# Second feed-forward of a two-block transformer: four pairs of weight chunks in seven products instead of three, their weight sums kept in DRAM

## What is computed

```
def sq_relu_mlp(h, w1, w2):                     # first block
    return jnp.square(jax.nn.relu(h @ w1)) @ w2
...
        merged = jax.nn.sigmoid(ga) * (y_a @ w_up_a[layer]) + jax.nn.sigmoid(gb) * (y_b @ w_up_b[layer])
        x = x + merged @ w_out[layer]
        h = rmsnorm(x, norm_ffn[layer])
        x = x + (jax.nn.silu(h @ w_gate[layer]) * (h @ w_up[layer])) @ w_down[layer]
    return rmsnorm(x, norm_final)
```

## Time and profile before

| | us |
|---|---|
| median of 3 runs | 718.4 (718.36 to 718.87) |
| the profiled execution | 718.42 |
| its span | 716.3 |
| TensorE busy / VectorE / ScalarE / GpSimd | 706.7 / 574.6 / 429.9 / 34.5 |

### The profile page before, as it was taken

How to read it: one execution, slowest core, us unless ns; L and a number is a source line. 1 busy time by engine, 2 the same in 40 slices (tenths; PEclk the granted TensorE clock), 3 DMA queues, 4 the chain that set the end, 5 groups by cost and what they waited for, 6 DMA issues and landing times.

```text
span 716.3 us, 9684 instructions
## 1 busy us (share of the span) xinstructions
PE 706.7 (99%) x3710; PEld 565.7 (79%) x3710; DVE 574.6 (80%) x972; ACT 429.9 (60%) x704; POOL 34.5 (5%) x55
## 2 busy tenths in 40 slices
PE   8999999999999999999999999999999999999996
PEld 4678885578888888888888777777888888888885
DVE  4789999899677868686998799855857789888883
ACT  3477658996745635646545677767447654754652
POOL 1030012001100100000010000000000000000000
PEclk9999999999999999999999999999999999999999
DMA  9996939617778975747538533336463894976901
GB/s 368 414 374 222 389 102 358 230 59 262 272 246 311 337 281 203 258 154 291 164 113 295 209 118 118 118 130 214 128 234 128 315 329 169 332 258 227 354 2 59
DMA packets 72109, 163.76 MB, mean 229 GB/s; under 512 B 4272, under 2 KB 15536, under 8 KB 70528
## 3 DMA queue, kind: packets, MB, share of 16 engines
q1 hardware_dynamic: 68016, 149.47, 58.8%
q0 software_dynamic: 3760, 13.42, 5.2%
q10 hardware_dynamic: 288, 0.27, 0.1%
HBM read 157.90 MB, written 5.24 MB: 228 GB/s over the span
## 4 chain that ended last, share of the span: by engine, by line
PE 95%; issue 1%; DVE 1%; ACT 1%; POOL 0%; POOLq 0%; DVEq 0%
PE bank L570 23%; PE bank L572 23%; PE bank L571 23%; PE bank L915 6%; PE bank L552 5%; PE bank L913 3%; PE bank L589 1%; PE bank L644 1%; PE bank L652 1%; PE bank L647 1%; PE bank L1047 1%; PE bank L1069 1%; PE bank L753 1%; PE bank L629 1%; PE bank L775 1%
## 5 line engine op out<-in xcount | busy, mean ns | idle before, releaser
L1791 DVE TENSOR_TENSOR WL<-W,WH 128x1024 fp32r<-128x1024 f32 (+2 forms) x240 | 270.4, 1172 | 25.6 <-ACT WH L1247 25.2
L1247 ACT ACTIVATE WH<-W 128x1024 fp32r<-128x1024 f32 (+2 forms) x240 | 228.6, 1013 | 63.4 <-DMA W<-in_w_mlp 38.1
L570 PE MATMUL bank<-WH,AHL 128*128 128x512 f32 (+1 forms) x420 | 165.2, 393 | 0.0
L572 PE MATMUL bank<-WH,AHL 128*128 128x512 f32 (+1 forms) x420 | 162.0, 386 | 0.0
L571 PE MATMUL bank<-WL,AHL 128*128 128x512 f32 (+1 forms) x420 | 161.8, 385 | 0.0
L570 PEld LDWEIGHTS bank<-WH,AHL 128*128 128x128 f32 x420 | 78.9, 188 | 18.2 <-issue 3.2
L572 PEld LDWEIGHTS bank<-WH,AHL 128*128 128x128 f32 x420 | 78.9, 188 | 16.2
L571 PEld LDWEIGHTS bank<-WL,AHL 128*128 128x128 f32 x420 | 79.1, 188 | 14.7
L570 PE MATMUL bank<-WH,HH 128*128 128x512 f32 (+1 forms) x218 | 84.8, 389 | 0.0
L572 PE MATMUL bank<-WH,HL 128*128 128x512 f32 (+1 forms) x218 | 84.5, 388 | 0.0
L571 PE MATMUL bank<-WL,HH 128*128 128x512 f32 (+1 forms) x218 | 84.4, 387 | 0.0
(11 more groups left out here) (311 smaller groups left out, 978.5 us busy)
## 6 DMA issues: line engine op xcount, KB each, us to landing
W<-in_w_mlp SPq DMA_DIRECT2D x32, 1024.0 KB, 5.9
W<-in_w_in SPq DMA_DIRECT2D x24, 1024.0 KB, 5.5
W<-in_w_down SPq DMA_DIRECT2D x11, 1024.0 KB, 5.3
W<-in_w_ada SPq DMA_DIRECT2D x10, 1024.0 KB, 8.3
WX<-in_w_ada SPq DMA_DIRECT2D x10, 1024.0 KB, 10.2
W<-in_w_up SPq DMA_DIRECT2D x9, 1024.0 KB, 6.2
W<-in_w_out SPq DMA_DIRECT2D x8, 1024.0 KB, 5.3
W<-in_w_gate SPq DMA_DIRECT2D x8, 1024.0 KB, 5.8
```

Source lines behind the costliest of these rows:

```text
L570: e.matmul(po, hs, wh[:, k, c0:c0 + cw], start=first and k == 0, stop=False, skip_group_check=onto)
L572: ins = e.matmul(po, ls, wh[:, k, c0:c0 + cw], start=False, stop=last and k == unit.nk - 1, skip_group_check=onto)
L1247: e.activation(m.WH[unit.slot][:, c], m.W32[unit.slot][:, c], ACT.Copy).then_inc(S["w_hi"], 1)
L1791: e.tensor_tensor(m.WL[unit.slot][:, c], m.W32[unit.slot][:, c], m.WH[unit.slot][:, c].bitcast(F32), ALU.subtract).then_inc(S["w_lo"], 1)
```

## The change

The pairs become chunks 2, 4, 6 and 9, so that three pairs follow each other directly and the last group is a pair too. The first three are stored, the last is made in place. The steps of stored sums go from 4 to 12: nine in the first block's feed-forward (places 0 to 6 take 2, 1, 2, 1, 1, 1, 1), one at place 7, one at place 9 and one at place 11. Where a pair follows a pair (`NEAR`), DVE makes the low parts of the next group's first two units before the third result sum. In the last group the projection down of the group before for token half 1 moves behind product 6.

```
-PAIRS = (2, 5, 8)
-STORED = (2,)
-STEPS = (4, 0, 0)
-SUMS_AT = (1, 0, 1, 0, 0, 0, 2, 0, 0, 0, 0, 0, 0)
+PAIRS = (2, 4, 6, 9)
+STORED = (2, 4, 6)
+STEPS = (9, 1, 2)
+SUMS_AT = (2, 1, 2, 1, 1, 1, 1, 1, 0, 1, 0, 1, 0)
...
+NEAR = [g for g in range(NG - 1) if GROUPS[g][1] and GROUPS[g + 1][1]]
...
-DN_ORDER = [(g, tb) for g in range(NG - 2) for tb in range(2)] + [(NG - 2, 0), (NG - 1, 0), (NG - 2, 1), (NG - 1, 1)]
+DN_ORDER = [(g, tb) for g in range(NG) for tb in range(2)]
...
+            if phase == 2 and i == 1:
+                power(10)
             w.wait_ge(S["made"], 4 * s + 4)
...
     kept_sums(1)
-    power(10)
+    kept_sums(2)
     power(11)
...
+        g = NG - 1
         for n, (c0, cw) in enumerate(LAST[1]):
-            part(by["dn", NG - 1][0], m.HH[(NG - 1) % 2], m.HL[(NG - 1) % 2], 0, 1, (1, 4, 5)[n], n > 0, True, "dn_mm",
-                 lambda k: ("hid_lo", 16 + 2 * NG), c0, cw)
+            for i, unit in enumerate(by["dn", g]):
+                part(unit, m.HH[g % 2], m.HL[g % 2], 2 * i, 1, (1, 4, 5)[n], n > 0 and i == 0, i == 1, "dn_mm",
+                     lambda k: ("hid_lo", 16 + 2 * NG), c0, cw)
...
-        down2(g - 1, 1, False, False)
+        if g < NG - 1:
+            down2(g - 1, 1, False, False)
...
-    up2(NG - 1, 1)
-    down2(NG - 2, 0, False, False, (0,))
-    for tb in range(2):
-        hid_turn2(NG - 1, tb)
-    down2(NG - 2, 0, False, False, (1,))
-    down2(NG - 1, 0, False, True)
+    rest(NG - 1)
+    hid_turn2(NG - 1, 0)
     down2(NG - 2, 1, False, False, (0,))
     down2(NG - 2, 1, False, True, (1,))
+    down2(NG - 1, 0, False, True, (0,))
+    hid_turn2(NG - 1, 1)
+    down2(NG - 1, 0, False, True, (1,))
     down2_last()
```

ScalarE's group with a pair:

```
-        hi(5)
-        hi()
+        near, final = g in NEAR, g == NG - 1
+        hi(4 if g - 1 in NEAR else 5)
+        hi(2 if near else 1)
         w.wait_ge(S["gu_mm"], QUAD_AT[g] + 6)
         w.wait_ge(S["hid2"], HID_AT[g - 1, 0])
         e.activation(m.rel[0][:, :], bank[4][:, :], ACT.Silu).then_inc(S["silu"], 1)
         hi()
+        if final:
+            hid_hi2(g, 0)
         w.wait_ge(S["quad"], 5 * q + 5)
         w.wait_ge(S["hid2"], HID_AT[g - 1, 1])
         e.activation(m.rel[1][:, :], m.g1[:, :], ACT.Silu).then_inc(S["silu"], 1)
...
+        if near:
+            hi()
+            hid_hi2(g, 0)
+            hi()
...
+        hid_hi2(g, 1)
```

VectorE's group with a pair (the result sums and `hidden` are the instructions of before, now in functions):

```
-        tt(m.u0, bank[6][:, :], m.g1[:, :], ALU.add, "quad")
-        lo(2)
-        w.wait_ge(S["gu_mm"], QUAD_AT[g] + 5)
-        tt(m.u1, bank[6][:, :], m.u1, ALU.add, "quad")
...
         if near:
-            first_hidden()
...
+            lo()
+            second_sum()
+            lo(4)
+            third_sum()
+            fourth_sum()
+            lo()
+            hidden(0)
+            fifth_sum()
+            lo()
+            hidden(1)
             hid_lo2(g, 0)
+            hid_lo2(g, 1)
+        elif final:
+            second_sum()
+            lo(3)
+            third_sum()
+            fourth_sum()
+            lo()
+            hidden(0)
+            fifth_sum()
+            hid_lo2(g, 0)
+            hidden(1)
             lo()
             hid_lo2(g, 1)
...
-            w.wait_ge(S["dn_mm"], DN_AT[NG - 1, tb] - 1 + n)
+            w.wait_ge(S["dn_mm"], DN_AT[NG - 1, tb] - 2 + 2 * n)
```

More of the change, by code:

```diff
@@ L1713, in quad_group @@
         e.activation(m.rel[1][:, :], m.g1[:, :], ACT.Silu).then_inc(S["silu"], 1)
-        if not GROUPS[g + 1][1]:
+        if near:
+            hi()
+            hid_hi2(g, 0)
+            hi()
+        elif not final:
             hi(2)
[L1716 to L1719, removed]
+            hid_hi2(g, 0)
+        hid_hi2(g, 1)
     silu_gate(0, 0)
@@ L1750, in scalar_program @@
                 hid_hi2(g, tb)
[L1751 to L1755, removed]
+    quad_group(NG - 1)
     def last_squares(tb):
@@ L2563, in quad_group, with product, first_sum, second_sum @@
         q = quads.index(g)
-        made, following, near = in_place(g), in_place(g + 1), GROUPS[g + 1][1]
+        made, near, final = in_place(g), g in NEAR, g == NG - 1
+        following = not final and in_place(g + 1)
+        def product(n):
+            w.wait_ge(S["gu_mm"], QUAD_AT[g] + n)
+        def first_sum():
+            product(2)
+            w.wait_ge(S["quad_act"], q + 1)
+            if q:
+                w.wait_ge(S["hid2"], HID_AT[quads[q - 1], 1])
+            tt(m.u1, bank[5][:, :], m.g1[:, :], ALU.add, "quad")
+        def second_sum():
+            product(3)
+            tt(m.u0, bank[6][:, :], m.g1[:, :], ALU.add, "quad")
+        def third_sum():
+            product(5)
+            tt(m.u1, bank[6][:, :], m.u1, ALU.add, "quad")
+        def fourth_sum():
+            product(4)
+            w.wait_ge(S["quad"], 5 * q + 2)
+            tt(m.u0, bank[5][:, :], m.u0, ALU.add, "quad")
+        def fifth_sum():
+            product(7)
+            tt(m.g1[:, :], bank[6][:, :], m.g1[:, :], ALU.add, "quad")
+        def hidden(tb):
+            w.wait_ge(S["hid_turned"], 4 + 2 * (g - 2) + 2)
+            w.wait_ge(S["silu"], SILU_AT[g, tb])
+            w.wait_ge(S["quad"], 5 * q + 4)
+            tt(m.hid[g % 2][:, tb, :], (m.u0, m.u1)[tb], m.rel[tb][:, :], ALU.mult, "hid2")
         if made:
@@ L2567, in quad_group @@
         lo()
[L2568 to L2572, removed]
+        first_sum()
         if made:
@@ L2575, in quad_group @@
         lo()
-        w.wait_ge(S["gu_mm"], QUAD_AT[g] + 3)
-        tt(m.u0, bank[6][:, :], m.g1[:, :], ALU.add, "quad")
-        lo(2)
-        w.wait_ge(S["gu_mm"], QUAD_AT[g] + 5)
-        tt(m.u1, bank[6][:, :], m.u1, ALU.add, "quad")
[L2581 to L2593, removed]
-        if near:
-            first_hidden()
-        w.wait_ge(S["gu_mm"], QUAD_AT[g] + 7)
-        tt(m.g1[:, :], bank[6][:, :], m.g1[:, :], ALU.add, "quad")
-        if following:
-            make(g + 1, 1)
-        lo()
-        if not near:
-            first_hidden()
-        w.wait_ge(S["silu"], SILU_AT[g, 1])
-        tt(m.hid[g % 2][:, 1, :], m.u1, m.rel[1][:, :], ALU.mult, "hid2")
-        if near:
-            hid_lo2(g, 0)
+        if near:
+            lo()
[8 more added lines that the diff above has]
+            hidden(1)
+            hid_lo2(g, 0)
+            hid_lo2(g, 1)
[9 more added lines that the diff above has]
+            hidden(1)
             lo()
             hid_lo2(g, 1)
-            lo()
-        else:
+        else:
+            second_sum()
+            lo(2)
+            third_sum()
+            lo()
+            fourth_sum()
+            if following:
+                make(g + 1, 0)
+            lo()
+            fifth_sum()
+            if following:
+                make(g + 1, 1)
+            lo()
+            hidden(0)
+            hidden(1)
             lo(2)
```

10 lines of the change are left out of this document (1 added, 9 removed).

## The result

| | before | after |
|---|---|---|
| median, us | 718.5 (718.36 to 718.87, 4 runs) | 746.0 (744.42 to 748.18, 4 runs) |
| ratio | | 1.038, 95% interval 1.036 to 1.041 |
| the profiled execution; its span | 718.42; 716.3 | 744.42; 742.6 |

A forecast was written before the change was run, and what follows sets the result against it. The prediction took TensorE's matmul work to bound the kernel: 2.7 us saved by fewer matmuls, against waits of 4.0, 2.1, 1.5, 3.7, 0.9 and 1.8, gave +11.3 on 718.42, so 729.7 us; range 720 to 734.5.

The forecast's parts named there:

- `up_wide(3)`: First block's feed-forward: TensorE waits 1.4 us for bank 4, which VectorE's late sum_wide(2) frees at 230.7.
- `up_wide(4)`: step 4's reload: First block's feed-forward: step 4's buffer is back about 244 to 246 for a wanted 245, so 0.6 us was added.
- chunks 3 to 6, up to `up_wide(7)`: First block's feed-forward: VectorE takes 20.5 us per chunk, leaving TensorE 4.0 us late in all at gate_sum.
- place 9: At the merge: the step heads a VectorE run without idling, so TensorE waits 2.1 us at merged_turn(0); bounds 1.5 and 3.5.
- product 6, first pair: Second feed-forward: product 6 waits 1.5 us for the third result sum, now behind low parts of the next pair.
- product 6, second pair: Second feed-forward: the same wait, with the second of two loads landing later: 3.7 us.
- hand-overs: From pair to pair: hidden(1) waits for the second down unit's high and low parts, 0.45 us each, 0.9 for both.
- last pair: Last group: low parts delay the third sum, 1.0 us, then hidden, 0.8: 1.8 us in all; bounds 0 and 3.
- transfers pile up: Rival: in three adjacent pairs each load takes 1 to 2 us longer, adding 4 us: 733.7; chance 0.10.
- VectorE's wait at place 1: First block's feed-forward: VectorE arrives near 212.5 and waits some 10 us for step 2's reload, landing at 222.8.
- A reload that lands early: Rival: store and load take 4 to 5 us each, so the first block's feed-forward costs nothing: 725.7; chance 0.12.
- VectorE's lateness never reaches TensorE: Rival: VectorE's 4 to 8 us free per chunk takes up the added work, only matmuls count: 715.7; chance 0.12.

The follow-up runs named there:

- e1_spread: Changed kernel with the second step of place 2 moved to place 6, so each step from number 4 on sits one place later: 733.4 us, ratio 1.020.
- e8: Changed kernel storing only 8 of 512 columns in the first four stores, first pair's units reading w_ada1 instead; reloads and arithmetic kept: 734.1 us, ratio 1.020.
- e12: Changed kernel with the arithmetic of all twelve steps cut to 8 of 512 columns, all reloads and stores kept: 726.7 us, ratio 1.012.
- e2_near: Changed kernel with the third result sum after two low parts, not four, where a pair follows a pair: 746.8 us, ratio 1.037.
- e3_place8: Changed kernel with the step of place 9 made in place 8, by the transfers of phase 1: 749.5 us, ratio 1.043.
- e9_nosteps_order: Changed kernel without its twelve steps, with low parts, third sums and hidden(1) reordered in the pairs: 722.9 us, ratio 1.006.

## Why the prediction was wrong

Term by term, in us of span, working as in the prediction:

| term | forecast | measured |
|---|---|---|
| fewer matmuls | -2.7 | -2.7: in the second feed-forward the records are 12 fewer, counted in 512 columns, at the same spacing |
| `up_wide(3)` | 1.4 | 2.1 |
| `up_wide(4)`: step 4's reload | about 1 | 8.1 |
| chunks 3 to 6, up to `up_wide(7)` | 1.6, the rest of 4.0 | 2.3 |
| half clock, `up_wide(4)` | none | 2.7 |
| places 7, 11 | 0 | 0.5 |
| place 9 | 2.1 | 2.1 |
| product 6, first pair | 1.5 | 1.1 |
| product 6, second pair | 3.7 | 3.5, and 2.7 of half clock |
| hand-overs | 0.9 | about 0.5, all of it at the first |
| last pair | 1.8 | 1.6 |
| the rest: ahead of the first block's feed-forward 0.6, behind the last matmul 0.6, small breaks 0.5 | none | 1.7 |
| sum | 11.3 | 26.2 |

- **The step that failed** is "step 4's buffer ... is back about 244 to 246 for a wanted 245, so I add 0.6". Its order of events was right: store, reload, store, reload, all in one queue. But it took 9 us for each store and 5.7 for the reload. In the trace they took 12.3, 13.0 and 10.1, which is 3.3 + 4.0 + 4.4 = 11.7 more, less 0.9 by which the first of them was issued sooner than forecast (216.9, not 217.8). So it was 254.4 where I had 244 to 246, and VectorE waited 7.9. I had a price measured in one queue position and used it for three transfers in a row: the two stores of the kernel before had no reload of their queue directly ahead (9.7 and 8.7 us), these two had. The forecast was early for every execution traced, since the lowest of eight landings is 250.3. e1_spread shows that this reload costs the 8 us: with the step moved away from it the wait is gone. e8 shows that it is late by the stores. In e12 the reload landed at 245.2, where I had it, and the wait at `up_wide(4)` did not come.
- **The bounds were too narrow for that.** I widened them by "a microsecond longer" each; a chain of three serial transfers adds its errors, and the upper bound for the block should have been some 10 us higher. The rival "transfers pile up" was the right mechanism at the wrong place: I priced it in the pairs, where product 6 came within 0.4 us of the forecast.
- **The clock was no term at all.** The earlier trace rows had 1.00 everywhere in the kernel before, and I took that for a constant. In that kernel TensorE never waited, and I did not ask what follows where it does. After two of the waits it was at half, 5.4 us in all.
- **Right**: the pace of VectorE between `sum_wide(3)` and `sum_wide(6)`, 61.9 us from 261.45 to 323.31 where 62.7 were forecast (3 x 20.5 and 1.2); VectorE's wait at place 1 (12.2 for 10); place 9 to 0.1 us; both product 6 waits. The hand-overs came to about half (my terms there add up to 8.75 us and not 8.9): the first cost 0.5 us over what the turns cost before, the second nothing. The place of the last loss of the block was not `gate_sum`, which did not wait for VectorE, but `up_wide(7)` behind `gate_add`, one item further down both queues.
- **The other rivals.** A reload that lands early is out: step 2's was issued at 216.2 and VectorE began at 224.1, 7.9 later, where the earlier trace rows has 5.7. That VectorE's lateness never reaches TensorE holds in the kernel before with four steps, and nearly in e12 (0.4 us at `up_wide(7)` is its longest wait in that block); with twelve full ones it does not.

The Trainium skill ("DMA: Bandwidth & Descriptors", Anatomy of one DMA) gives by its fit an estimate of 4.4 us for each 1 MB store; the trace has 9.6, 12.3 and 13.0 in this stretch. The same page (Issuing engines are not separate DMA queues) says that transfers issued by different engines run on the same 16 DMA engines and interleave; a share of 0.99 to 1.01 while SyncE's weight loads and GpSimd's stores ran side by side fits that, though no run here takes the loads away.

What stays open: why the clock fell after a wait of 2.0 us at `up_wide(3)` in e1_spread and not after 1.9 us at the same place in the changed kernel; why the same reload took 4.9 us in one execution and 12.3 in another; how much of the 12.3 and 13.0 us is the place behind the reloads and how much the full DMA engines; and where the 0.6 us behind the last matmul comes from.

## What to carry to other kernels

A wait on an engine with spare time is free until the spare time is used up; then extra work shows, so add up an engine's work and its waits over a whole stage and compare with the stage's length, not with one point in it. A transfer's price from one place does not hold for several in series behind each other in one queue under a full DMA load: take the sum's bound from the slowest landing seen. And where TensorE has never waited, count a new wait of 2 us or more with the chance of a stretch at half the clock behind it (up to 2.8 us here).

## What the runs showed of the hardware

**A wait can cost twice.** After 3.3 us of waiting at product 6 of the second pair, the next dozen matmuls started 0.43 us apart and not 0.23 (TensorE, and a window):

```profile
637.94 0.79 PE L571 MATMUL bank<-WH,AHL 128*128 128x512 f32 x1 [3.27 <-DVE g1b L1803]
638.53 0.63 PE L572 MATMUL bank<-WL,AHL 128*128 128x512 f32 x1
638.96 0.63 PE L573 MATMUL bank<-WH,AHL 128*128 128x512 f32 x1
639.39 0.63 PE L571 MATMUL bank<-WH,AHL 128*128 128x512 f32 x1
```

```profile
638.00:644.00 6.00, 6.00 (x15) 4.70 (x16) 3.89 (x5) 0.39 (x1) 0.00 (x0) 0.52 0.81 319
```

In e1_spread a wait of 3.0 us at the same place left the clock at 1.00. Over all the traces the clock fell behind waits as short as 1.8 us (e2_near, at 616.1) and stayed at 1.00 behind others of up to 3.4 (e3_place8, at 644.4), so the wait's length alone does not tell. The Trainium skill ("TensorE: Matmul & The Clock Gate", What's actually happening) says that the clock follows how busy TensorE has been; the drops behind waits agree with that.

**Kernels with waits scatter more.** The kernel before stays within 1.5 us over all its runs. e8_small_store gave 728.65 at a mean clock of 0.997, and 736.24, 735.3 and 732.93 at 0.992, 0.990 and 0.991. (1 - clock) x span, the time lost to the clock if TensorE is busy, is 2.2 us in the first and 5.9 to 7.3 in the others, so half to all of the 4.3 to 7.6 us between them is the clock's. e9_nosteps_order, whose waits are of 1.4 us at most, stays within 0.7 us.

**A 1 MB store from GpSimd's queue has no one price.** From issue to the next instruction on the queue it took 5.8 us in e12_small_steps (issued at 204.2, DMA share 0.74) and 9.6 in the changed kernel (issued at 205.85, share 0.94 from 206 to 216), 1.6 us later at the same point of the program. The share does not settle it either: in the kernel before one took 9.7 us at a share of 0.99, in the changed kernel the one behind two reloads 12.3 at the same share. Rows of e12, the store and what waits for it, and the window:

```profile
204.21 0.76 POOL L480 DMA_DIRECT2D sums<-sums  x1 [18.23 <-DVE sums L1803]
210.05 0.71 POOL L467 DMA_DIRECT2D sums<-in_w_up  x1 [5.08 <-DMA sums<-sums]
```

```profile
204.00:210.00 6.00, 6.00 (x36) 5.18 (x35) 2.37 (x6) 2.78 (x4) 0.76 (x1) 1.00 0.74 225
```
